# Gate/up bias of the experts as float32 one-hot products in four row groups, and one weight place loaded in two pieces before the others

## What is computed

```python
def moe_ffn(h, router_w, router_b, w_gate_up, b_gate_up, w_down, b_down):
    t = h.reshape(bsz * s, d)
    logits = (t @ router_w + router_b).astype(jnp.float32)
    top_v, top_i = lax.top_k(logits, TOP_K)
    top_w = jax.nn.softmax(top_v, axis=-1)
    combine = jnp.einsum('tk,tke->te', top_w, jax.nn.one_hot(top_i, N_EXPERTS, ...))
    for e in range(N_EXPERTS):
        a = clamped_swiglu(t @ w_gate_up[e] + b_gate_up[e])
        out = out + combine[:, e:e + 1] * (a @ w_down[e] + b_down[e])
```

## Time and profile before

| | us |
|---|---|
| median of 3 runs | 1255.19 |
| lowest and highest | 1254.52, 1256.24 |
| the profiled execution | 1255.92 |
| its span in the profile | 1254.2 |

### The profile page before, as it was taken

One profiled execution on the slowest core, in us unless ns is written; L12 is line 12 of the kernel. 1 busy time (PEld: TensorE's weight loads), 2 busy tenths in 40 slices (PEclk: granted clock), 3 DMA queues, 4 the chain that ended last, 5 costly groups with the idle time before them and its releaser, 6 DMA issues.

```text
span 1254.2 us, 16244 instructions
## 1 busy us (share of the span) xinstructions
PE 1188.3 (95%) x6634; PEld 623.2 (50%) x6634; DVE 441.4 (35%) x869; ACT 286.3 (23%) x514; POOL 112.9 (9%) x97
## 2 busy tenths in 40 slices
PE   7999999999999999999998989898999989899996
PEld 7999988788843434434342424343333333243432
DVE  6886666767431231312121222212221212122212
ACT  5683448653410101101010101010110101010112
POOL 2311312444500000000000000000000000000000
PEclk9999999999999999999999999999999999999999
DMA  7747434329999999999999999999999999999995
GB/s 225 226 136 245 155 106 146 122 79 353 380 425 428 428 431 433 433 431 430 430 434 434 432 431 431 432 433 434 431 431 431 433 434 434 428 432 431 425 427 230
DMA packets 60252, 453.57 MB, mean 362 GB/s; under 512 B 9000, under 2 KB 33712, under 8 KB 45104
## 3 DMA queue, kind: packets, MB, share of 16 engines
q1 hardware_dynamic: 59904, 452.75, 87.8%
q10 hardware_dynamic: 304, 0.20, 0.1%
HBM read 451.88 MB, written 1.05 MB: 361 GB/s over the span
## 4 chain that ended last, share of the span: by engine, by line
PE 63%; DMA 29%; ACT 3%; DVE 3%; issue 1%; POOL 0%; SPq 0%; DVEq 0%; ACTq 0%
PE psum L1243 23%; DMA ring<-in_w_gate_up_dram 14%; DMA slot<-in_w_gate_up_dram 12%; PE psum L1253 10%; PE psum L882 9%; PE psum L1219 5%; PE psum L844 4%; PE psum L1279 3%; PE psum L801 3%; DMA ring<-in_w_down_dram 3%; PE psum L885 2%; ACT WH L1408 1%; DVE WL L1715 1%; ACT XDT L1582 1%; PE psum L1129 1%
## 5 line engine op out<-in xcount | busy, mean ns | idle before, releaser
L1243 PE MATMUL psum<-ring,ZS 128*64 128x512 f32 x1520 | 347.8, 601 | 14.1 <-DMA ring<-in_w_gate_up_dram 13.5
L1243 PEld LDWEIGHTS psum<-ring,ZS 128*64 128x64 f32 x1520 | 106.7, 137 | 218.4 <-issue 199.4
L2202 DVE TENSOR_TENSOR X<-X,psum 128x1024 f32<-128x1024 f32 x62 | 72.9, 1218 | 373.2 <-PE psum L1279 373.1
L1253 PE MATMUL psum<-ring,HT 128*64 128x512 f32 x736 | 168.2, 610 | 23.1 <-DMA ring<-in_w_down_dram 23.1
L1243 PE MATMUL psum<-slot,ZS 128*64 128x512 f32 x512 | 118.1, 605 | 11.2 <-DMA slot<-in_w_gate_up_dram 11.2
L2184 DVE TENSOR_SCALAR ZS<-psum 128x512 f32<-128x512 f32 x32 | 22.1, 692 | 299.7 <-PE psum L1243 299.7
L1253 PEld LDWEIGHTS psum<-ring,HT 128*64 128x64 f32 x736 | 57.5, 140 | 126.5 <-issue 124.8
L1715 DVE TENSOR_TENSOR WL<-ring,WH 128x2048 fp32r<-128x2048 f32 (+1 forms) x43 | 98.4, 2291 | 43.0 <-ACT WH L1408 42.7
L1632 ACT ACTIVATE HT<-psum 128x512 f32<-128x512 f32 x31 | 18.5, 597 | 316.4 <-PE psum L801 316.4
L1408 ACT ACTIVATE WH<-ring 128x2048 fp32r<-128x2048 f32 (+1 forms) x43 | 80.8, 1878 | 14.5 <-PE psum L844 6.8
L1243 PEld LDWEIGHTS psum<-slot,ZS 128*64 128x64 f32 x512 | 34.8, 138 | 79.0 <-issue 59.8
(11 more groups left out here) (369 smaller groups left out, 1204.5 us busy)
## 6 DMA issues: line engine op xcount, KB each, us to landing
ring<-in_w_gate_up_dram SPq DMA_DIRECT2D x38, 4096.0 KB, 29.4
ring<-in_w_down_dram SPq DMA_DIRECT2D x18, 4096.0 KB, 30.7
slot<-in_w_gate_up_dram SPq DMA_DIRECT2D x12, 4096.0 KB, 28.9
ring<-in_w_gate_up_dram SPq DMA_DIRECT2D x19, 2048.0 KB, 13.5
ring<-in_w_in_dram SPq DMA_DIRECT2D x30, 1024.0 KB, 5.3
slot<-in_w_down_dram SPq DMA_DIRECT2D x7, 4096.0 KB, 30.8
ring<-in_w_down_dram SPq DMA_DIRECT2D x10, 2048.0 KB, 16.7
slot<-in_w_gate_up_dram SPq DMA_DIRECT2D x8, 2048.0 KB, 15.4
```

The lines of the kernel that those rows point to most:

```text
L1243: ins = mm(psum[64 * (c % 2):64 * (c % 2) + 64, c // 2, :], XTS[:, k, s], every_other_run(w[:, at:at + 2048], c), start=False, stop=(k == ...
L1253: ins = mm(psum[64 * h:64 * h + 64, 2, :], lhs, w[:, at:at + 512], start=(k == 0), stop=(k == 7))
L2202: v.tensor_tensor(xo, xo, psum[:, 3 + 2 * t:5 + 2 * t, :], ALU.add).then_inc(o_read, 1)
```

## The change

- The bias is kept in float32 (`BGX`, 4 x 32 partitions by 1024): four loads instead of six, piece c on partitions 32 c to 32 c + 31. GpSimd's splitting goes.
- `OHE` becomes float32 with 128 partitions. Each of the four products of `bias` reads 32 rows, its own row group, and writes the same place as before.
- The two products at 1187 become four float32r products of 256 columns from HTH.
- `once` is loaded in two pieces of 1 MB: quarter 1 (in YV) directly after the last load of the units, quarter 0 (in XC) after `mt_full` 4. TensorE waits for both where it reads them.
- To make room, `H2T` moves to ZS and `WFF` and the bias to KD. `WFF` is loaded after the last scores (`sc_full` 16) without waiting for `bs` 3.

```diff
--- before.py
+++ after.py
@@ -278,7 +278,6 @@
         HID = sb("HID", [P, 2, GROUPS, 16])
         BDK = sb("BDK", [P, GROUPS, 2, 16])
         AMX = sb("AMX", [P, 3, 4, 4])
-        OHE = sb("OHE", [P, 2, CAP], BF16)
 
 
 
@@ -330,13 +329,13 @@
         PTS = part(XDT, 2048, 2, 512)
         MG = GA[:, :, 0:D]
         H2 = part(XC, 0, T, D)
-        H2T = part(XC, 2048, KT, SEQ)
-
-        WFF = part(YV, 0, D)
+        H2T = part(ZS, 0, KT, SEQ)
+
+        WFF = part(KD, 1024, D)
         WFN = part(YV, 0, D)
         WFNR = UPP[0:8]
-        BGF = [part(KD, 1024, D), part(YV, 1024, D)]
-        BG3 = at_place("BG3", [P, 2048], kd_at, BF16)[:]
+        BGX = part(KD, 0, D)
+        OHE = part(CM, 0, 2, CAP)
         UST16 = at_place("UST16", [P, P], pr_at + 4 * 64, BF16)[:]
         IDB = part(PR, 0, EXPERTS)
         WFC = part(PR, 32, KT)
...
@@ -547,13 +546,11 @@
                     sp.wait_ge(gm_ready, 8)
                     sp.dma_start(WFNR, final_norm_w.rearrange("(b c) -> b c", c=P)
                                  ).then_inc(late_in, 16)
-                    sp.wait_ge(unit_done, at_unit[("bs", 3)] + 1)
+                    sp.wait_ge(sc_full, 16)
                     sp.dma_start(WFF, ffn_norm_w[0].partition_broadcast(P)).then_inc(late_in, 16)
-                    sp.wait_ge(sc_full, 16)
-                    for c in range(2):
-                        for r in (0, 32, 64):
-                            sp.dma_start(BGF[c][r:r + EXPERTS, :], b_gate_up[0][:, D * c:D * c + D]
-                                         ).then_inc((bg_in, bg_in2)[c], 16)
+                    for c in range(4):
+                        sp.dma_start(BGX[32 * c:32 * c + EXPERTS, :], b_gate_up[0][:, D * (c // 2):D * (c // 2) + D]
+                                     ).then_inc(bg_in, 16)
                 if kind == "small":
                     v = slot_view(u, KT, 64)
                     sp.dma_start(v[:, :, 0:16], w_cols(w_in, OFF_DT, 16)).then_inc(full, 16)
@@ -587,14 +584,22 @@
                     return gate_up_rows(nxt if h else e + 2, n - 3)
                 return down_rows(e + (2 * h + 1))
 
+            def once_quarter(q):
+
+                part_of = slice(SLOT * q, SLOT * q + SLOT)
+                sp.dma_start(once[:, part_of], unit_rows(3, 0, 4)[:, HALF:BIG][:, part_of]).then_inc(once_full, 16)
+
             def early_load(unit, hi):
                 load_half(unit_rows(unit, 0, 4), LOOP_SLOT[unit], hi)
 
+            once_quarter(1)
             sp.wait_ge(unit_done, at_unit[("bn", 3)] + 1)
             load_half(gate_up_rows(0, 1), 1, 0)
             low_ready(sp, len(SPLIT_UNITS) - 3)
             low_ready(sp, len(SPLIT_UNITS) - 2)
             early_load(0, 1)
+            sp.wait_ge(mt_full, 4)
+            once_quarter(0)
             sp.wait_ge(unit_done, at_unit[("wo", 1)] + 1)
             early_load(1, 0)
             low_ready(sp, len(SPLIT_UNITS) - 4)
@@ -604,10 +609,6 @@
             early_load(1, 1)
             sp.wait_ge(unit_done, NU)
             load_half(gate_up_rows(0, 1), 1, 1)
-            sp.wait_ge(bias_ready, 1)
-            sp.wait_ge(rt_full, T)
-            sp.wait_ge(h2_ready, 4)
-            sp.dma_start(once, unit_rows(3, 0, 4)[:, HALF:BIG]).then_inc(once_full, 16)
             for n, (unit, hi) in enumerate(((2, 0), (2, 1), (3, 0), (7, 1))):
                 sp.wait_ge(unit_done, NU + n + 1)
                 early_load(unit, hi)
@@ -742,31 +743,18 @@
             pool.wait_ge(ht_full, 1)
             own.mark(g.tensor_copy(ONE16[:], ONE[:]))
             own.mark(g.tensor_copy(UST16, UST[:]))
-            own.mark(g.tensor_tensor(IDB[0:96], IDN[0:96, 0:32], IDN[0:96, 32:64], ALU.add))
+            own.mark(g.tensor_tensor(IDB, IDN[:, 0:32], IDN[:, 32:64], ALU.add))
             own.settle()
-            own.mark(g.tensor_tensor(IDB[0:96], IDB[0:96], IDN[0:96, 64:96], ALU.add))
-
-            for c in range(2):
-                if c:
-                    low_ready(pool, SPLIT_UNITS.index(at_unit[("wo", 2)]))
-                pool.wait_ge((bg_in, bg_in2)[c], 16 * 3)
-                wide, terms = BGF[c], BG3[:, D * c:D * c + D]
-                own.mark(g.tensor_copy(terms[0:96], wide[0:96]))
+            for r in (64, 96):
+                own.mark(g.tensor_tensor(IDB, IDB, IDN[:, r:r + 32], ALU.add))
                 own.settle()
-                own.mark(g.tensor_tensor(wide[0:96], wide[0:96], terms[0:96], ALU.subtract))
-                own.settle()
-                own.mark(g.tensor_copy(terms[32:64], wide[32:64]))
-                own.settle()
-                own.mark(g.tensor_copy(terms[64:96], wide[64:96]))
-                own.settle()
-                own.mark(g.tensor_tensor(terms[64:96], wide[64:96], terms[64:96], ALU.subtract))
-                own.settle()
+            pool.wait_ge(nm_ready, 16)
+            own.mark(g.tensor_copy(OHE, IDB[:, 0:2].unsqueeze(2).to_broadcast([P, 2, CAP])))
+            own.settle()
+            pool.sem_inc(bias_ready, 1)
+
             for m in range(4):
                 cols = slice(256 * m, 256 * m + 256)
-                if m == 2:
-                    own.mark(g.tensor_copy(OHE[0:96], IDB[0:96, 0:2].unsqueeze(2).to_broadcast([96, 2, CAP])))
-                    own.settle()
-                    pool.sem_inc(bias_ready, 1)
                 pool.wait_ge(x2_ready, m + 1)
                 if m < 2:
                     xv, wv = (x[:, 0:512].rearrange("p (c k) -> p k c", k=4) for x in (X[:, m], WFF))
@@ -1178,16 +1166,19 @@
 
             def bias(s):
                 for c in range(4):
-                    mm(psum[64 * (c % 2):64 * (c % 2) + 64, c // 2, :], OHE[0:96, s],
-                       every_other_run(BG3[0:96], c), start=True, stop=False)
+                    r = slice(32 * c, 32 * c + EXPERTS)
+                    runs = BGX[r].rearrange("p (m h e) -> p h m e", h=2, e=8)[:, c % 2]
+                    mm(psum[64 * (c % 2):64 * (c % 2) + 64, c // 2, :], OHE[r, s], runs, start=True, stop=False,
+                       tile_position=(32 * c, 64 * (c % 2)))
 
             def warm(n):
 
                 for _ in range(n):
-                    mm(psum[:, 7, :], ONE16[0:96], BG3[0:96, 0:512], start=True, stop=True)
+                    mm(bank(7, SEQ), HTH[:, 0, 0:P], HTH[:, 1, :], start=True, stop=True)
 
             pe.wait_ge(bias_ready, 1)
-            warm(2)
+            pe.wait_ge(bg_in, 16 * 4)
+            warm(4)
             pe.wait_ge(msk_ready, 1)
             mm(bank(3, EXPERTS), UST16, MSK[:, 0], start=True, stop=True).then_inc(rk_full, 1)
             bias(0)
@@ -1225,7 +1216,7 @@
 
                 slot = LOOP_SLOT[unit]
                 if isinstance(i, int) and i == 0 and (unit, hi) == (3, 1):
-                    pe.wait_ge(once_full, 16)
+                    pe.wait_ge(once_full, 16 * 2)
                     return once_hi
                 if isinstance(i, int) and i == 0:
                     pe.wait_ge(half_full[slot][hi], early_loads(unit, hi))
@@ -2162,7 +2153,7 @@
                 v.tensor_copy(C2[:, 0], SLT[:, :, cols]).then_inc(dve_own, 1)
                 v.tensor_copy(C2[:, 1], CW[:, :, cols]).then_inc(dve_own, 1)
                 if not first:
-                    v.tensor_copy(OHE[0:96], IDB[0:96, cols].unsqueeze(2).to_broadcast([96, 2, CAP])
+                    v.tensor_copy(OHE, IDB[:, cols].unsqueeze(2).to_broadcast([P, 2, CAP])
                                   ).then_inc(dve_own, 1)
                     dve.wait_ge(dve_own, base + 3)
                     slots_of(C2[:, 0]).then_inc(dve_own, 1)
```

More of the change, by code:

```diff
@@ L392, in hybrid_block @@
          at_full, at_ready, zero_ready, cw_ready, gn_read, sq2_ready, bd_in, spr_ready, wh_ready,
-         wl_ready, ys_high, ys_ready, ht_low, mt_low, ot_high, bg_in, bias_ready, rw_ready, wo_half, wfn_ready, bg_in2, wide_half, rs_ready, h2n_ready, wfn_full, mix_in, mix_full, mix_ready, smf_ready, smt_full, sqs_ready) = [sem(n) for n in (
+         wl_ready, ys_high, ys_ready, ht_low, mt_low, ot_high, bg_in, bias_ready, rw_ready, wo_half, wfn_ready, wide_half, rs_ready, h2n_ready, wfn_full, mix_in, mix_full, mix_ready, smf_ready, smt_full, sqs_ready) = [sem(n) for n in (
             "rows_in small_in late_in const_done dve_own act_own pool_own hn_ready ht_full ht_act "
@@ L405, in hybrid_block @@
             "bd_in spr_ready wh_ready wl_ready ys_high ys_ready ht_low mt_low ot_high bg_in bias_ready "
-            "rw_ready wo_half wfn_ready bg_in2 wide_half rs_ready h2n_ready wfn_full mix_in mix_full mix_ready smf_ready smt_full sqs_ready").split()]
+            "rw_ready wo_half wfn_ready wide_half rs_ready h2n_ready wfn_full mix_in mix_full mix_ready smf_ready smt_full sqs_ready").split()]
         loads = {u: 2 if UNITS[u][0] == "small" else 1 for u in range(NU)}
```

## The result

| | us |
|---|---|
| before, median of 20 runs | 1255.44 (1254.16 to 1256.52) |
| after, median of 20 runs | 1257.1 (1256.41 to 1258.45) |
| ratio after / before | 1.0015, 95% interval 1.0010 to 1.0021 |
| span of the profiled execution, before and after | 1254.2, 1255.5 |

The kernel became slower by about 1.7 us, where 0.9 us of gain was forecast. 1257.1 us lies in the outer range of the prediction, but above the forecast's own (1252.3 to 1256.5) and on the other side of no change. Three single executions among those of the experiments, of 1737, 2000 and 3107 us, stand far apart from all others and are left out of the comparisons. The profiled spans differ by 1.3 us, so the trace shows most of what there is to explain.

The account below looks back on a forecast made before the run. The weight stream was taken to bound the kernel. The least gate saving, 0.6 us (1.1 with a shorter empty-queue time), taken as 0.9, gave 1255.0 profiled and 1254.3 median; range 1251.9 to 1261.1, the forecast's own 1252.3 to 1256.5.

Parts of the forecast that it names:

- What bounds the kernel: From about 280 us the weight stream sets the pace, 431 GB/s at 500 to 700; TensorE has 3.3 us spare a pair.
- The transfer that moves: Stream at 305 to 320 us: each 1 MB piece of `once` fits a hole almost whole; 4.9 us leave the busy part.
- What is late next, the first gate: Load behind expert 0's first finished quarter: 1.8 of its 9.6 us are queue; less 0.37, 1.4 us saved.
- The first loads of 4 MB: Loads issued at 436.1 and 445.4: slack 3.1 and 3.5 us over 12.7; after bias delays 0.8 and 0.6 saved.
- The bias price: Each expert's bias products: four at a time plus 0.21 for tiling, 1.06 us on TensorE's chain, 0.63 more than before.
- B: Rival, chance 0.14: only two of four bias products run at a time, 1.92 us a bias; slower by 6.0, 1261.2 us.
- C: Rival, chance 0.06: bias products sharing a PSUM bank take turns, 2.8 us a bias, 2.3 more; 1267 us.
- The chain of gates: Gates up to the first 4 MB loads: each later bias adds 0.63 us until TensorE waits for weights; later covered.
- The tail: From before 1152.76 us on: three biases, 1.9 us, just fit into 2.16 us of TensorE's waits, adding nothing.
- The rest at nothing: Two fewer bias transfers, GpSimd's splitting gone, one-hot tile filled earlier, changed addresses: no effect on the time.

Follow-up runs that it names:

- whole-loop halves: Every load of the loop issued as two 2 MB halves: on after 1261.93 us, ratio 1.0055; on before 1260.22 us, ratio 1.0045.
- `once` late: After, but `once` loaded whole at its old place in SyncE's order: 1256.66 us against 1255.1 for before, ratio 1.0014.
- old-cost bias: After, with four bf16 bias products of 96 rows as before, three-term split left out: 1254.94 us against 1255.1 for before, ratio 1.0001.
- bias twice: After, with each bias product issued twice, the repeat starting the sum anew: 1260.2 us, ratio 1.0038 against before.

## Why the prediction was right or wrong

**What bounds the kernel: right.** The end follows the stream. In every kernel without whole-loop halves the shift of the last landing and that of the span agree within 0.4 us (after +1.3 and +1.3, `once` late +0.7 and +0.6, old-cost bias -0.9 and -0.9, bias twice +4.1 and +4.0).

**The transfer that moves: right.** The pieces were issued at 294.8 and 311.7 and the holes took them in. They didn't reach the 400 GB/s that I had named (374 and 392). From 280 to 340 us the stream moved 384 GB/s against 355, 1.74 MB more, 4.0 of the 4.9 us.

**What is late next, the first gate: wrong in size.** The mechanism was seen: a window far below 300 GB/s (82), and an issue at 344.14, which is 0.25 earlier than before only because everything in this execution ran about 0.5 us earlier already at 268 us. The failed step is the reading of "So only 1.8 us of the 9.6 are queue" as a saving that lasts. The load landed 2.7 earlier, but most of that did not last, and landings and bytes moved do not shift together. Counted in bytes, after has gained 60 x 29 = 1.74 MB up to 340 and lost 1.85 MB up to 346: 0.11 MB behind, with 0.26 MB fewer to bring (the two bias transfers). (0.26 - 0.11) / 0.431 = 0.35 us was saved, not 1.4. The landings come close to this in the end: of the 2.7 us 1.5 are lost again in one step, between the landings at 361.2 and 367.5 (6.4 us apart, where 4.9 is the pace of 2 MB), and 1.2 stand before the loop, 0.5 of them the offset of the execution. That step belongs to the early `once`: it stands in all eight kernels that have it (at 357 to 363 with the bias twice), 1.2 to 1.6 us beyond the pace, and in none of the four that load `once` late (0.7 at most). Against the kernel with the same bias and `once` late the load at the gate landed 1.9 us ahead (351.4, not 353.3), about the 1.8 that had been forecast before the bias was taken off; behind the step 0.4 of it is left (367.5, not 367.9). Why the step comes was not tested.

**The first loads of 4 MB: wrong, and this decided the sign.** The failed step is "an empty queue would give 7.8 + 4.9 = 12.7 us". The delay of the gates was forecast well: 0.37 + 3 x 0.63 = 2.3 us at the first, where the issue is 1.8 later and the whole execution 0.5 earlier. But the loads took 14.7 and 14.9 us, so of the slack of 3.1 and 3.5 only about 1.1 and 1.3 could be used. It is not that 12.7 was too low as the time into an empty queue: with the bias twice the first 4 MB load is issued at 441.20 and lands 12.0 us later. The fault is to take a stream as full until a landing time has come down to that of an empty queue; it ran thin while 3 to 5 us of transfers still lay ahead. Against a delay of 1.8 us in the issue at 437.9 the stretch runs thin, as the windows show: 407 GB/s with the bias long and `once` early, 418 with `once` late, 430 to 432 with the short bias, with none, or with halves. How much the stream has in hand is told by a load's lead: how long it is issued before the landing of the load ahead. Before: 442.2 - 436.1 = 6.1 and 451.9 - 445.4 = 6.5 us, and the next landing follows 9.7 us later, the pace of 4 MB at 431 GB/s. After: 3.3, 4.6 and 7.4, with 11.4, 10.3 and 10.4. The prediction took 12.7 - 9.7 = 3.0 us of lead as enough. It is no sharp limit: leads of 3.6 and 2.1 us in two other kernels lost only 0.4 and 0.2, one of 3.7 lost 2.3, one of 4.7 nothing, while the leads of 5.3 to 7.2 us of the first two such loads in the kernels with the short bias or none lost nothing at all. That the thin stretch follows the bias and goes with halves is shown; the threshold is not, nor why the stream runs thin with transfers still queued.

**The bias price: right in mechanism, near in size.** 0.73 us against 0.63, eight instructions on the chain, 1.02 us against 1.06. The 0.1 more lies in the quarter behind it (3.58 for 3.44), which the sum had not. Rivals B (1.92) and C (2.8) fell: the 1.02 us holds though two products write one bank each. C rested on a sentence of the Trainium skill ("TensorEngine Tiling (Array Packing)", Restrictions and Gotchas), that different row tiles can't access one PSUM bank at a time; by this trace it doesn't hold as a cost for row groups that write different partitions of a bank. The 3.07 times of the Trainium skill ("TensorE: Matmul & The Clock Gate", Part 3) gave an estimate of 1.11 us, and the trace shows 1.02: 3.3 times by the estimated 3.41.

**The chain of gates: half right.** That the early biases add up ahead of the loop and are covered later is what the kernels without and with doubled bias show. The subtraction used the right biases and a slack of which 1.1 to 1.3 us could be used, not 3.1 to 3.5.

**The tail: right.** The wait near 1226 is gone, and the tail adds nothing: +1.3 us at 1154 and +1.3 at the end. With the bias at 1.9 us the tail does cost, 1.3 of the 2.7 us by which that kernel's trace is longer than after's.

**The rest at nothing: right.** The two kernels that keep one part apart add up to after within 0.3 us (1.6 - 0.2 against 1.7), less than their intervals.

**The forecast.** Of its two ends, a gain at the first gate of 1.4 us and a remainder of 0.6 to 0.8 at the loop, the first was 0.35 and the second negative. No rival had this: B names the same path (the stream thin behind the gates) with a bias price that isn't there. The rival that was missing is the forecast's own price with a stream that runs thin before its queue is empty. That 1257.1 lies in the outer range at all is luck: the range reaches up there only for B, whose bias price fell. And the prediction held 0.2% (2.5 us) for about what can't be told from no change; 20 executions of each told 1.7 us apart, with an interval of 1.0010 to 1.0021.

**Open.** The landings of after are 1.2 us ahead at 432 us, 2.1 behind at about 485, 2.9 behind at 513, and 1.3 to 1.4 behind from 521 to the end. The window 434 to 475 explains 2.4 of the first 3.3. The last turn is not a gain of after but a step of 1.6 us in the landings of the kernel before, between 510.1 and 521.4 us, with no dip in its rate that would explain it. The same kernel with its loop's first round written out has no step there (9.7 us, 510.0 to 519.7). Besides the step of the early `once` at 361 to 367, steps of 1.1 to 1.6 us stand between 1140 and 1194 in four other kernels. Most of these stretches hold a fetch of 16 KB of TensorE's instructions; but the kernel before has such a fetch at 361 to 363 too, and no step there. The cause of none of them was tested. It means that a single pair of traces tells about 1 us at best, and that here the medians and their intervals carry the verdict.

## What to carry to other kernels

In a stream of gated loads the slack of a gate is not the landing time less that of one load into an empty queue: look at the lead, from a load's issue to the landing of the one ahead, and at the rate window around the gate. A transfer taken out of the queue ahead of a gate gives only what the gate doesn't hold back, counted in bytes moved by both kernels up to the first time past the gate. A few tenths of a microsecond on the engine that opens the gates count several times over before the backlog builds up, and not at all after.

## What the runs showed that I had not expected

- Loads of 2 MB move 427 to 428 GB/s in a full stream, loads of 4 MB 431 to 432. In the kernel before, all loop loads in halves cost 5.1 us, more than anything else in this study.
- The first 4 MB loads of after were issued 3.3 and 4.6 us before the load ahead had landed, and still landed 11.4 and 10.3 us behind it, where 9.7 us is the pace in a full queue.
- A transfer taken out ahead of a gate did bring the next landing forward (1.9 us against the kernel with the same bias and `once` late), and some 15 us later one step gave 1.5 us of it back.
- Four float32 tiles of 32 rows by 64 columns run side by side, two of them in one PSUM bank: 8 instructions of 587 to 639 ns each in 1.02 us.
- Writing out one more round of the loop (37 fetches of 16 KB of instructions instead of 32, in the two kernels on after) cost 1.4 us on before and 1.6 on after. That the fetches themselves are the cost was not shown.
